# Gate and up units of four feed-forward networks: two matmuls per block of x where there were three, and an add on VectorE

## The reference, cut to what matters

```
def swiglu(h, w_gu, w_down):
    gate, up = jnp.split(h @ w_gu, 2, axis=-1)
    return (jax.nn.silu(gate) * up) @ w_down

x = x + 0.5 * swiglu(rms_norm(x, norm_ffn1[i]), w_ffn1_gu[i], w_ffn1_down[i])
```

## Time and profile before

| what | value |
|---|---|
| median of three runs | 3046.54 us (3046.16 to 3047.29) |
| the profiled execution: its own time | 3044.58 us |
| its span, first to last instruction | 3042.8 us |
| PE busy | 2690.4 us, 88% of the span |
| DVE busy | 2014.6 us, 66% |
| ACT busy | 1321.0 us, 43% |
| chain that ended last | PE 54%, DMA 10%, DVE 9%, issue 3%, ACT 3% |

### The profile page before, as it was taken

The page is one execution under the profiler, slowest core; times in us unless marked ns, Lnnn a source line. Parts: engine busy times, 40 slices in busy tenths (PEclk is TensorE's granted clock), DMA queues, the critical chain, the costliest instruction groups (busy, mean ns, idle before and its releaser), DMA issues.

```text
span 3042.8 us, 44796 instructions
## 1 busy us (share of the span) xinstructions
PE 2690.4 (88%) x14826; PEld 2179.4 (72%) x14826; DVE 2014.6 (66%) x3711; ACT 1321.0 (43%) x2261; POOL 859.9 (28%) x1227
## 2 busy tenths in 40 slices
PE   8998799999989979999999679999896787887776
PEld 8987599889879966899999558888776333333322
DVE  6665467667656754567778985555685777777664
ACT  4445544444434444454445754455553222222221
POOL 3432344235324400111000641100001343444442
PEclk9999899999999998999999879999998899999999
DMA  9974199789859951799755019965544999999997
GB/s 344 362 267 152 56 333 369 243 303 361 296 207 375 340 181 64 252 333 345 264 182 183 0 55 353 349 236 193 193 144 135 382 416 414 417 411 412 406 421 304
DMA packets 198902, 841.04 MB, mean 276 GB/s; under 512 B 27552, under 2 KB 27552, under 8 KB 165136
## 3 DMA queue, kind: packets, MB, share of 16 engines
q0 software_dynamic: 99760, 479.01, 40.7%
q1 hardware_dynamic: 99040, 360.75, 33.7%
HBM read 771.49 MB, written 135.27 MB: 298 GB/s over the span
## 4 chain that ended last, share of the span: by engine, by line
PE 54%; DMA 10%; DVE 9%; issue 3%; ACT 3%; POOL 1%; DVEq 0%; ACTq 0%; POOLq 0%
PE ps L1515 15%; PE ps L1516 15%; PE ps L1517 15%; DMA arena<-both_rows,arena 10%; PE ps L1884 6%; DVE arena L1390 2%; DVE first_hot L1458 1%; PE ps L1663 1%; PE ps L1561 1%; DVE second_hot L1461 1%; DVE w_lo L911 1%; DVE arena L1470 1%; ACT arena L663 0%; DMA both_rows<-arena 0%; ACT arena L544 0%
## 5 line engine op out<-in xcount | busy, mean ns | idle before, releaser
L911 DVE TENSOR_TENSOR w_lo<-raw,w_hi 128x1024 fp32r<-128x1024 f32 x681 | 831.5, 1223 | 625.9 <-ACT w_hi L509 619.8
L509 ACT ACTIVATE w_hi<-raw 128x1024 fp32r<-128x1024 f32 x681 | 719.6, 1057 | 664.2 <-PE ps L1517 371.9
L1515 PE MATMUL ps<-act_hi,w_hi 128*128 128x256 f32 x2728 | 780.3, 286 | 5.8 <-DVE act_lo L945 4.0
L1516 PE MATMUL ps<-act_lo,w_hi 128*128 128x256 f32 x2728 | 773.7, 284 | 0.0
L1517 PE MATMUL ps<-act_hi,w_lo 128*128 128x256 f32 x2728 | 773.5, 284 | 0.0
L1884 PE MATMUL ps<-arena 128*128 128x512 f32 x1024 | 490.8, 629 | 154.8 <-ACT arena L663 154.8
L1515 PEld LDWEIGHTS ps<-act_hi,w_hi 128*128 128x128 f32 x2728 | 524.9, 192 | 15.7 <-issue 9.8
L1516 PEld LDWEIGHTS ps<-act_lo,w_hi 128*128 128x128 f32 x2728 | 525.1, 192 | 5.8 <-issue 2.6
L1517 PEld LDWEIGHTS ps<-act_hi,w_lo 128*128 128x128 f32 x2728 | 525.1, 192 | 0.0
L1884 PEld LDWEIGHTS ps<-arena 128*128 128x128 f32 x1024 | 195.1, 199 | 438.7 <-ACT arena L663 230.4
L1390 DVE SCALAR_TENSOR_TENSOR arena<-arena 128x1024 f32<-128x1024 f32 x256 | 313.5, 1225 | 184.2 <-DMA arena<-both_rows,arena 182.5
(11 more groups left out here) (243 smaller groups left out, 3049.2 us busy)
## 6 DMA issues: line engine op xcount, KB each, us to landing
raw<-in_stream SPq DMA_DIRECT2D x684, 512.0 KB, 5.2
arena<-in_stream POOLq DMA_DIRECT2D x128, 512.0 KB, 8.8
both_rows<-arena POOLq DMA_DIRECT2D x512, 128.0 KB, 5.9
both_rows<-in_stream POOLq DMA_DIRECT2D x128, 512.0 KB, 5.9
pad<-in_ln POOLq DMA_DIRECT2D x4, 1024.0 KB, 6.1
arena<-both_rows,arena POOLq DMA_INDIRECT x256, 10.8
arena<-in_subkeys POOLq DMA_DIRECT2D x2, 1024.0 KB, 5.5
x<-in_x SPq DMA_DIRECT2D x1, 1024.0 KB, 5.0
```

The source lines that it names most:

```text
L509: act.activation(w_hi[:, u % SPLIT, :], raw[:, u % RAW, :], ACT.Copy).then_inc(hi_done, 1)
L911: dve.tensor_tensor(w_lo[:, u % RAW, :], raw[:, u % RAW, :], w_hi[:, u % SPLIT, :].bitcast(F32), ALU.subtract).then_inc(lo_done, 1)
L1515: pe.matmul(dst, lhs[0], rhs[0], start=first, stop=False, **kw)
L1516: pe.matmul(dst, lhs[0], rhs[1], start=False, stop=False, **kw)
```

## The change

The two parts of x become halves of one tensor, `act_both`. For a gate or up unit the three matmuls per block become two: the high weights once, with 512 columns moving (high x, then low x) into a whole PSUM bank, and the low weights with the 256 columns of high x, added onto the second half of the bank. So a bank holds high by high in its first half and the two cross terms in its second; gate lies in bank 4 or 6, up in bank 5 or 7. The halves have to be added: ScalarE copies the second halves of both banks to on-chip memory (`gate_up_low`), VectorE adds the first halves (`gate_up_sum`), ScalarE takes silu of the sum, VectorE multiplies. The order on both engines is written out in the diff.

```
-        act_hi = in_place("act_hi", [P, KD, T], hots_at)
-        act_lo = in_place("act_lo", [P, KD, T], hots_at + 4 * KD * T)
+        act_both = in_place("act_both", [P, 2, KD, T], hots_at)
+        act_hi, act_lo = act_both[:, 0], act_both[:, 1]
...
+        gate_up_sum, gate_up_low = blk(A_FFN + 8 * T, 2, 2 * T), blk(A_FFN + 12 * T, 2, 2 * T)
...
                 def chunk(s, units_after=1):
                     act.wait_ge(unit_used, t.value(unit_used) + units_after)
-                    act.activation(silu[:, s, :], ps[:, 4 + s, 0:T], ACT.Silu).then_inc(silu_done, 1)
+                    act.activation(gate_up_low[:, s, :].rearrange("p (n t) -> p n t", n=2),
+                                   ps[:, 4 + 2 * s:6 + 2 * s, T:2 * T], ACT.Copy).then_inc(low_kept, 1)
+                    act.wait_ge(sum_ready, t.after(sum_ready))
+                    act.activation(silu[:, s, :], gate_up_sum[:, s, 0:T], ACT.Silu).then_inc(silu_done, 1)
                     split()
                     act.wait_ge(h_ready, t.after(h_ready))
...
                 def chunk(s, units_after=2):
+                    dve.wait_ge(low_kept, t.after(low_kept))
+                    dve.tensor_tensor(gate_up_sum[:, s, :].rearrange("p (n t) -> p n t", n=2),
+                                      ps[:, 4 + 2 * s:6 + 2 * s, 0:T],
+                                      gate_up_low[:, s, :].rearrange("p (n t) -> p n t", n=2),
+                                      ALU.add).then_inc(sum_ready, 1)
+                    split()
                     dve.wait_ge(silu_done, t.after(silu_done))
-                    dve.tensor_tensor(prod[:, s, :], silu[:, s, :], ps[:, 4 + s, T:2 * T],
+                    dve.tensor_tensor(prod[:, s, :], silu[:, s, :], gate_up_sum[:, s, T:2 * T],
                                       ALU.mult).then_inc(h_ready, 1)
-                    split()
                     dve.wait_ge(h_hi_ready, t.after(h_hi_ready))
...
-                        ins = mm3(dst, w(s, P * k, P), a(k), k == 0, k == KD - 1)
+                        high, low = w(s, P * k, P)
+                        pe.matmul(ps[:, bank, :], high, act_both[:, :, k, :], start=k == 0, stop=k == KD - 1,
+                                  skip_group_check=True)
+                        ins = pe.matmul(ps[:, bank, T:2 * T], low, act_hi[:, k, :], start=False, stop=k == KD - 1,
+                                        skip_group_check=True)
```

More of the change, by code:

```diff
@@ L231, in program @@
         acc_kept = sem("acc_kept")
+        low_kept = sem("low_kept")
+        sum_ready = sem("sum_ready")
         silu_done = sem("silu_done")
@@ L580, in ffn @@
                 chunk(0, 2)
-                with t.loop(5, [(h_ready, 4)] + unit_steps(12)):
+                with t.loop(5, [(h_ready, 4), (sum_ready, 4)] + unit_steps(12)):
                     for j in range(4):
@@ L1576, in ffn, with features @@
             def ffn():
-                def features(dst, fresh=False):
+                def features(bank, fresh=False):
                     s = unit()
@@ L1582, in features @@
                             pe.wait_ge(act_ready, t.after(act_ready))
-                        ins = mm3(dst, w(s, P * k, P), a(k), k == 0, k == KD - 1)
+                        high, low = w(s, P * k, P)
[3 more added lines that the diff above has]
+                                        skip_group_check=True)
                     return ins
                 def gate_up(s, fresh=False):
-                    features(ps[:, 4 + s, 0:T], fresh).then_inc(unit_used, 1)
-                    features(ps[:, 4 + s, T:2 * T]).then_inc(unit_used, 1)
+                    features(4 + 2 * s, fresh).then_inc(unit_used, 1)
+                    features(5 + 2 * s).then_inc(unit_used, 1)
                 def down(s, last=False):
```

## The result

The changed kernel takes 3115.5 us (median of five, 3107.7 to 3115.8) against 3046.2 for the kernel before in the same comparison: the ratio is 1.0226, with a 95% interval of 1.0212 to 1.0240. It is slower by 69 us; 3118 was forecast.

What follows compares the result with a forecast made beforehand. TensorE was taken to bound the kernel, transfers close behind; a helper wait loop would take over. Network terms of +72.6 us less 0.8 gave +71.8 on the profiled 3044.6, so 3116, plus 2.0 for the median: 3118 us, range 3085 to 3136.

Steps and rivals of the forecast that it cites:

- The ring: ScalarE and VectorE wait for each other in series: 8.52 or 9.65 us per chunk, mean 9.09, against TensorE's 8.31; 83%.
- The add: VectorE's add of 128x512 with one operand in PSUM, taken at 0.69 us, bounds 0.61 and 1.30.
- slow bound of 1.30: Rival: VectorE's add costs 1.30 us like the row with scattered columns, +51 us, giving 3169 us; chance 5%.
- The table load: ScalarE's 1.28 us load at a network's start now begins behind the copy, ending 0.5 us after the add: +0.5.
- The last `down`: At each network's end TensorE idles 6.9 us, then runs twelve matmuls at low clock: 5.4 us to the add on x.
- The networks: First product to add on x: +15.9 us in the first network and +18.9 in three others, 72.6 in all.
- When TensorE starts to wait: Slack of at most 3.1 us, eaten at 0.78 per chunk; TensorE waits for `h_lo` after about four chunks or fewer.
- VectorE's gaps: VectorE idles until ScalarE's split: about 1.4 us ahead of a chunk's first split, about 1.1 ahead of the second.
- what TensorE is spared: Gate and up matmuls: 0.360 us per block becomes 0.348, 0.19 less per chunk, 16.5 us over 88 chunks.
- the fast rival: ScalarE and VectorE overlap, so TensorE's 8.31 us per chunk hold: 3041 us, or 3030 if ends cost nothing; chance 8%.
- rival 2: Transfers at 372 GB/s set the pace, 8.50 us per chunk, and only the ends cost: 3057 us; chance 4%.
- TensorE's waits: TensorE waits for `h_lo` in nearly every chunk from the fifth, some 70 us in all, four of about 7.

Runs made afterwards that it cites:

- wide matmuls alone: Changed kernel with the copy and add left out, silu and product reading the first halves of the banks, cross terms missing: 3033.4 us, 0.9965 of before.
- split first: Changed kernel with ScalarE's split moved from behind silu to between the copy and the wait for the add: 3040.9 us, 0.9984 of before.

## Why the prediction was right

- **The ring** was right as a mechanism, and its sum to 0.01 us: 8.52 and 9.65 us between adds, in all four networks (but for one of 9.72 and the first of each). That the sum is so exact is luck in part: add to silu measures 0.69 for the 0.73 of the sum, product to `h_hi` 0.45 for 0.42, silu to the high split 0.32 for 0.29, and these cancel. Opened on either engine, it vanished with all of its cost; lengthened by an add, it took 0.60 us more per chunk.
- **The add** was taken at 0.69 us and its row measures 0.65 (0.57 from its start to the next instruction's); the copy 0.58 for 0.60. The slow bound of 1.30 did not come up; that contiguous runs are the reason, as the prediction has it, was not tried.
- **The table load**: it starts when the copy ends (22.12, its silu starting at 23.41), and the first distance is 10.24 for 9.65 us, so +0.6 for the 0.5 of the sum. It fell out in the fourth network, where the trace has no table load and the distance is 9.69, so this term was 0.5 us too long there.
- **The last `down`**: TensorE waited 6.60 us for the forecast 6.9, and from it to the add on x it took 223.15 - 218.69 = 4.46 us in the first network and 5.5 in the other three, for 5.4. The clock was low there, as forecast, but in the first network it rose again halfway (below), which the sum did not have.
- **The networks**: +72.6 in the sum, +71.4 measured.
- **When TensorE starts to wait** was wrong, though nothing in the sum hangs on it. The slack of 3.1 us for some four chunks holds in the middle of the loop, where gate and up and a `down` (8.3 us) lie between; ahead of the first `down` there is only gate and up (5.6). In the first network `h_lo` of chunk 0 was done at 27.29 and TensorE took it at 28.17, and already the second `down`, at 37.06, waited 0.34 us.
- **VectorE's gaps**: 1.43 us ahead of the first split, for about 1.4. The 1.1 ahead of the second came as two gaps, 0.48 ahead of `h_lo` and 0.52 ahead of the split.
- **Mis-sized: what TensorE is spared.** The step took the wide matmul at 0.228 us and came to 16.5 us; it costs 0.2325 and the whole is 10.6. In the changed kernel this hardly shows, since the ring sets the pace, but it was wrong in the fast rival too, whose price of 3041 was met by the kernel with the ring open (3040.9) only by accident: the matmuls brought 6 us less than its sum had, and the ends cost some 7 us for its 10.8.
- **The rule on the gap.** The Trainium skill (TensorE: Matmul & The Clock Gate, Back-to-back issue gap) gives an isolated matmul's warm gap as its columns over 2.4 plus about 2.5 ns. An estimate worked out from that figure is that leaving out the third matmul spares 2.5 ns per block. Measured, 0.360 became 0.3525 us per block, 7.5 ns: between that estimate and the 13 ns that the rows of before suggested.
- **The transfers**: the share fell to 0.94 to 0.96, not to 0.92. They did not set the pace: with the wide matmuls alone it was 8.39 us throughout at a share of 0.98 to 0.99, and 3057 us (rival 2) did not come up.
- **TensorE's waits**: 63.2 us for some 70, in 43 waits rather than in nearly every chunk: a chunk with two transposes overshoots TensorE's 8.38 by 1.27 us and one with a single transpose by 0.14, so the row shows one wait per pair.

## What to carry to other kernels

When work is added between two engines that run in written order, don't compare its length with their idle time; walk once around the loop of hand-overs, from an instruction to its next occurrence, and compare that sum with the pace of the bounding engine. Here 1.2 us of added work on two engines that were busy for 70% and 45% made a loop of 9.09 us out of one that had fitted in 8.50, and moving one independent instruction ahead of the new wait brought it down to 7.0 and 8.1 with nothing taken away. What counts as independent has to be looked at on both sides. VectorE's first split stood ahead of its wait for silu and still closed the ring, because its input, ScalarE's split, stood behind silu; putting it back behind the product opened the ring as well.

## What the runs showed of the hardware that was not expected

A wide matmul (512 moving columns in two runs of 256, 8 KB apart) and a narrow one together took 0.353 us in the stream: with the wide matmuls alone, 0.236 from the wide one's start to the narrow one's and 0.117 from there to the next wide one's. With the narrow one at 0.120 as before, the wide one has 0.2325, where those with one run took 0.228; whether the two runs or the narrow neighbour cost the 4 ns was not tried apart. The clock after waits of the same length did not go alike. After 2.06 us it was low in three networks of four (above, split first). After 6.60 us, in the changed kernel, it came back in one of four. The last `down` of the first and of the second network as stretches (the column before the last two is the granted clock, 0.5 being 1.2 GHz):

```profile
218.60:223.20 4.60, 4.42 (x12) 3.23 (x12) 1.32 (x3) 0.53 (x1) 0.00 (x0) 0.66 0.16 51
601.90:607.50 5.60, 5.49 (x12) 3.80 (x12) 1.28 (x2) 0.46 (x1) 0.00 (x0) 0.51 0.09 31
```

In the first network the matmuls were 0.43 us apart up to 221.42 and 0.23 from 221.78 on, in the second, as in the third and fourth, 0.43 to the end. What decides it was not tried.
